# The last half of projection block E ahead of the first fox scores, in the two second mixers

## The reference, cut to what matters

```
proj = h @ w_in_2[l]                       # columns in blocks A, B, C, D, F, E
nsa:  8 heads, in two branches here (selected blocks; window), pairs 0..3 and 4..7
      s = q k^T / 8, causal; p = softmax(s); o = p v
nsa, compressed branch: kcmp, vcmp = gelu(blocks @ w1) @ w2
      s_cmp = q kcmp^T, masked softmax, o_cmp = p_cmp vcmp
fox:  4 heads, pairs 8 and 9:  s = q k^T / 8 + F_i - F_j   (F: running sum of log forget gates)
moba: 4 heads, pairs 10 and 11: s = q k^T / 8, causal
x = x + gate * (concat(o) @ w_out_2[l])
```

## Time and profile before

| what | us |
|---|---|
| median of three runs | 1502.72 (1501.37 to 1504.84) |
| the profiled execution, its own time | 1500.39 |
| its span, first to last instruction | 1498.6 |
| TensorE busy in the span | 1453.8 (97%) |
| VectorE busy | 1149.1 (77%) |
| ScalarE busy | 784.6 (52%) |

### The profile page before, as it was taken

The page is one execution under the profiler, slowest core; times in us unless marked ns, Lnnn a source line. Parts: engine busy times, 40 slices in busy tenths (PEclk is TensorE's granted clock), DMA queues, the critical chain, the costliest instruction groups (busy, mean ns, idle before and its releaser), DMA issues. The chain is left out here.

```text
span 1498.6 us, 20923 instructions
## 1 busy us (share of the span) xinstructions
PE 1453.8 (97%) x8376; PEld 1251.0 (83%) x8376; DVE 1149.1 (77%) x1607; ACT 784.6 (52%) x1115; POOL 26.3 (2%) x31
## 2 busy tenths in 40 slices
PE   8997999999899999999999999899999999999997
PEld 6885889998788887788798888888888787888886
DVE  6797788898779877676679987789878675787653
ACT  7546555764555533656465542555535664565541
POOL 0021000000000000000000000000000000000000
PEclk9999999999999999999999999999999999999999
DMA  8132377988468787433357769478696331466550
GB/s 348 57 105 103 110 270 273 367 335 314 166 246 352 282 289 267 159 122 113 113 189 291 307 261 351 161 308 316 234 337 232 134 137 61 141 250 234 191 183 28
DMA packets 57152, 327.19 MB, mean 218 GB/s; under 512 B 6608, under 2 KB 7120, under 8 KB 27600
## 3 DMA queue, kind: packets, MB, share of 16 engines
q1 hardware_dynamic: 55440, 322.76, 57.6%
q10 hardware_dynamic: 1616, 3.10, 0.6%
HBM read 324.78 MB, written 1.05 MB: 217 GB/s over the span
## 5 line engine op out<-in xcount | busy, mean ns | idle before, releaser
L335 DVE TENSOR_TENSOR wlo<-raw,whi 128x2048 fp32r<-128x2048 f32 (+2 forms) x236 | 533.5, 2264 | 87.7 <-ACT whi L328 86.7
L328 ACT ACTIVATE whi<-raw 128x2048 fp32r<-128x2048 f32 (+2 forms) x236 | 445.7, 1894 | 133.5 <-PE ps L1604 93.6
L1356 PE MATMUL ps<-hreg_r,whi 128*128 128x512 f32 x1504 | 359.5, 391 | 1.9 <-ACT whi L328 0.8
L1356 PEld LDWEIGHTS ps<-hreg_r,whi 128*128 128x128 f32 x1504 | 276.7, 188 | 56.3 <-ACT whi L328 1.0
L370 DVE CUSTOM_DVE_ANT_0 adaw<-adaw,crow,colp 128x1024 f32<-128x1024 f32 x144 | 182.8, 1280 | 38.9 <-DMA adaw<-in_wada 38.7
L1365 PEld LDWEIGHTS ps<-hreg_r,wlo 128*128 128x128 f32 x1504 | 192.5, 191 | 7.0
L1365 PE MATMUL ps<-hreg_r,wlo 128*128 128x256 f32 x1504 | 195.6, 283 | 0.0
L1533 ACT ACTIVATE mix<-ps 128x512 f32<-128x512 f32 x93 | 55.6, 598 | 218.4 <-PE ps L1365 215.7
L1596 PE MATMUL ps<-whi,ireg_r 128*128 128x512 f32 x416 | 129.9, 393 | 0.2 <-ACT ireg_r L1490 0.2
L1600 PE MATMUL ps<-wlo,ireg_r 128*128 128x512 f32 x416 | 128.3, 389 | 0.0
L1604 PE MATMUL ps<-whi,ireg_r 128*128 128x512 f32 x416 | 128.1, 389 | 0.0
(11 more groups left out here) (415 smaller groups left out, 1913.1 us busy)
## 6 DMA issues: line engine op xcount, KB each, us to landing
raw<-in_wu SPq DMA_DIRECT2D x182, 1024.0 KB, 5.7
adaw<-in_wada SPq DMA_DIRECT2D x144, 512.0 KB, 5.0
raw<-in_wx SPq DMA_DIRECT2D x48, 1024.0 KB, 5.5
raw<-in_wu SPq DMA_DIRECT2D x4, 568.0 KB, 5.6
raw<-in_wu SPq DMA_DIRECT2D x2, 544.0 KB, 5.5
x<-in_x SPq DMA_DIRECT2D x2, 512.0 KB, 4.1
out<-hreg SPq DMA_DIRECT2D x2, 512.0 KB, 2.7
crow<-in_c ACTq DMA_DIRECT2D x1, 512.0 KB, 7.8
```

What stands on the lines that cost most here:

```text
L328: act.activation(self.whi[:, m, 0:width], self.raw[:, n % NRAW, 0:width], ACT.Copy).then_inc(*self.A.done("hi", n))
L335: dve.tensor_tensor(self.wlo[:, m, 0:width], self.raw[:, n % NRAW, 0:width], self.whi[:, m, 0:width].bitcast(F32), ALU.subtract).then_inc( ...
L1356: pe.matmul(self.ps[:, b, :], self.whi[:, m, c:c + 128], self.hboth[:, kt], start=kt == 0, stop=False)
```

## The change

In each second mixer the call `chunk("E", 1, 1)` moves up by one call: it stood behind `scores(8)`, and now stands ahead of it, directly behind the products with the compressed keys. The whole diff:

```
         mm.then_inc(*P.done("cs", st))
+        chunk("E", 1, 1)
 
         scores(8)
-        chunk("E", 1, 1)
         turned_probs(7)
         values(7)
```

## The result

The changed kernel takes 1513.85 us (median of four runs, 1512.20 to 1514.82) where the kernel before takes 1502.71 us in the same rounds. The ratio is 1.0093, with a 95% interval from 1.0070 to 1.0115: slower. The medians are 11.1 us apart (a ratio of 1.0074), and the recorded ratio says 14.0 us; the record doesn't show where the two part, so the size is known to no better than that. Either is more than the 7.0 us forecast. The direction was as forecast, and the size was not.

A forecast was written before the change was run, and what follows sets the result against it. TensorE, busy 97% of the span, was taken as the bound. Wait 2.45 plus clock 1.05 us, times two mixers, gave +7.0 us on 1502.7: 1509.7 us, 0.47% slower, range 1505.4 to 1514.0.

The forecast's parts named there:

- the wait: Ahead of `values(7)`: late `scores(8)` delays ScalarE's copy, about 4.4 us idle, net 2.45 us lost a mixer.
- The difference of 1.57 us: The moved chunk: 2.85 us at full clock instead of 4.42 us, saving 1.57 us of TensorE time a mixer.
- The clock behind the new wait: At `values(7)` and `scores(9)`: the new idle time brings half clock, costing 1.05 us a mixer.
- The two terms for which I had no row: Half-clock cost of L2449, taken as +0.28 (bounds 0, +1.51), and `values(7)`, taken as 0 (bounds 0, +1.45).
- The wait without half clock: Rival ahead of `values(7)`: the wait comes, but the clock is full again; +4.9 us, 1507.6 us, chance 0.15.
- Half clock until the output projection: Rival behind the wait: clock stays low to the projection, 3.30 us more a mixer; +13.6 us, 1516.3 us, chance 0.07.
- The half clock of before: Rival at `scores(10)` to `turned_probs(9)`: their half clock comes earlier and disappears there; +2.4 us, 1505.1 us, chance 0.12.
- The faster case: Rival ahead of `values(7)`: no wait, only the chunk's better clock remains; 3.1 us less, 1499.6 us, chance 0.04.

The follow-up runs named there:

- filled: Changed kernel with 17 dummy products of 512 columns in the idle time ahead of `values(7)`: 1.0029 of the kernel before.
- copies_first: Changed kernel with VectorE doing emit(6) and probs(7) ahead of maxima(8), and ScalarE probs(7) ahead of exps(8): 0.9999 of the kernel before.
- small_filled: Changed kernel with 18 dummy products of 64 columns over 128 rows in the idle time ahead of `values(7)`: 1.0030 of the kernel before.
- after_full_rows: Changed kernel with the one-row products L2449 run over 128 rows, the added rows zeros: 1.0066 of the kernel before.
- dense_late: Changed kernel with 12 dense dummy products behind `values(7)`, ahead of `scores(9)`: 1510.84 us in one execution, no ratio.
- filled_8: Changed kernel with 8 dense dummy products in the idle time ahead of `values(7)`: 1.0080 of the kernel before.

## Why the prediction was wrong

**Right: the wait.** I said that `scores(8)` comes 2.85 us later, that ScalarE gives back 0.40 us, and that `values(7)` is 2.45 us late after some 4.4 us of idle time. Counted from the start of L2592, `values(7)` starts at 12.33 us (705.33 - 693.00) and started at 10.00 us before (705.83 less 695.83, the start of the stretch): 2.33 us late. The idle time is 4.21 us. The filled kernel shows the same term alone: 2.23 and 2.32 us in a mixer. The chunk ran at full clock and took 2.94 us (694.76 to 697.70; 2.85 said). One reading was loose: the 4.42 us of the chunk before are not all at half clock, which ended about 1 us before the chunk did. The difference of 1.57 us is measured, so the sum doesn't hang on it.

**Wrong: the step "The clock behind the new wait".** Its term was 1.05 us a mixer: L2445 +0.56, L2453 +0.21, L2449 +0.28, `values(7)` 0. What the first mixer of the changed kernel shows in its place is 7.32 - 2.33 = 4.99 us (the second, 6.88 - 2.32 = 4.56 us). Two rows of the kernel before are needed for its parts, the start of `turned_probs(8)` and that of `values(8)`:

```profile
709.88 0.82 PE L2461 MATMUL ps<-cst,ireg 128*128 128x128 f32 x6
...
712.41 0.43 PE L2475 MATMUL ps<-ireg 128*128 128x64 f32 x2 [1.27 <-DVE ireg L2851]
```

| from the start of | to the start of | before, us | changed, us | more |
|---|---|---|---|---|
| `values(7)` | `scores(9)` | 1.45 | 2.72 | 1.27 |
| `scores(9)` | `turned_probs(8)` | 2.60 | 4.84 | 2.24 |
| `turned_probs(8)` | `values(8)` | 2.53 | 2.67 | 0.14 |
| `values(8)` | `scores(10)` | 1.48 | 2.75 | 1.27 |
| `scores(10)` | output projection | 13.87 | 13.94 | 0.07 |

Three things follow.

- The two terms for which I had no row were near doubling: L2449 went from 1.51 to 2.85 us (+1.34; I took 0.28), and `values(7)` from 1.45 us to 2.72 us (705.33 to 708.05; +1.27, I took 0). L2445 went to 1.59 us (+0.74; I took 0.56), and L2453 to 0.40. Doubling was one bound of both terms; I stood at or near the other, arguing that these products are limited by something other than columns. Whatever limits them, it slowed with the clock. These rows make 3.51 of the 4.99 us.
- Half clock did not end with `scores(9)`. It held over the transposes and `values(8)` too, and through `scores(10)` to about 722 us. I had priced one round of the pipeline. The transposes behind `scores(9)` and `values(8)`, at half clock now and at full clock before, cost 1.41 us. This is what is left after a wait that shrank: ahead of `values(8)` it fell from 1.27 to 0.33 us, where I had said that it takes nothing back. From `scores(10)` on there was half clock before as well, and it cost 0.07 us more.
- Its cause was only in part the one I gave. I tied it to the idle time alone. The profiled execution of copies_first has 0.34 us of idle time and just as much half clock; the same 4.21 us of idle time with full rows leave 7.1 us of it. But the medians show that the idle time counts: without it the typical execution has 34 us of half clock in place of 56.

**What the clock depends on, as far as shown.** Three things take the added half clock away: work in the idle time, dense or small (filled, small_filled: 56 to 27 us in the typical execution); the copies ahead, which remove the idle time (copies_first: 34 us); and 128 rows for the one-row products with the idle time left as it is (after_full_rows: 33 us, and 17.3 to 7.1 us in the first stretch). So neither the idle time nor the one-row products alone make the long half clock of the typical execution; here it took both. None of the three is a clean removal of idle time: filling adds products, and copies_first also alters two engines' orders and brings `values(7)` nearer to the scores of pair 8. Dense products at the place behind `values(7)` bring the clock back (dense_late, one execution). What stays open is why one program goes both ways: 1.00 and 0.86 in the two mixers of filled_8, 0.982 to 0.992 in the twelve executions of copies_first. Something beyond the order of the products and the length of the idle time decides it, and no run here tells what.

The rule that I drew on, from the Trainium skill, "TensorE: Matmul & The Clock Gate", Part 1, has two halves. That sustained activity brings the clock back agrees with dense_late, where the clock went from 0.50 to 1.00 over the twelve dense products. That idle time takes it down agrees with the medians, 56 us of half clock with 4.21 us of idle time and 34 us with 0.34. The profiled execution of copies_first, at half clock while TensorE was busy for 98% of the time, shows that idle time is not all of it.

**The rivals.** The wait without half clock (+4.9 us) is what the filled kernel measures, +4.3 us, and not what the changed kernel did. "Half clock until the output projection" had 7 in 100 and 1516.3 us; the ratio of 1.0093 on 1502.7 us gives 1516.7 us. By the medians the change cost 11.1 us, not 14.0. If the rival's size was right, that was luck. Most of the 3.30 us a mixer that it added did not come: `scores(11)` and the projection were at full clock, and all behind the start of `scores(10)` cost 0.07 us more. The doubled small products and `values(8)` made up for that. The half clock of before did not go elsewhere. The faster case fell as argued, with the wait in its place.

**The range.** Its upper end of 1514.0 us left out the rival with the long half clock and cut off the upper bound of the forecast's own two unknown terms, 1515.1 us. The median of 1513.85 us lies just inside, the 1516.7 us of the ratio outside.

## What to carry to other kernels

Before moving a dense block of products in a hand-written pipeline, look for two jobs that it may have: it covers a chain on the other engines, and it may hold TensorE's clock up among small products. The first is read from the idle time of the other engines ahead of the work that the block delays; the second from the granted clock around it, which a busy share does not tell.

Where a trace has no row for a product at half clock, price it at double: here even the 64-column products (1.45 to 2.72 us) and the one-row products (1.51 to 2.85 us) took about 1.9 times as long.

Products over one row of the array can cost more in clock than in time. Filling the unused rows with zeros cost nothing that the profile shows and made the kernel before 0.26% faster (0.9974, 0.9955 to 0.9994). With the copies ahead it gained nothing that can be told.

Don't rest a reading of the clock on one profiled execution. That of copies_first was the lowest of twelve, and alone it would say that the idle time is harmless.

## What the hardware showed unexpectedly

In one execution TensorE stayed at half clock for over 16 us while it was busy for 16.01 of 16.40 us (copies_first). Eighteen products of 64 columns in the idle time kept the clock as well as seventeen of 512 columns (median clock 0.991 with either). Over eight executions, zero rows under the one-row products raised the clock of the changed kernel from 0.9815 to 0.989, though they were no faster themselves. And the clock of one and the same sequence differs inside one execution, 1.00 and 0.86 in the two stretches of filled_8, and between executions, 0.982 to 0.992 in copies_first.
